# A routed feed-forward kernel: the activations of the first seven experts are computed in the routing block

## The reference, cut to what matters

```python
q = (xt @ w_q).reshape(n, PEER_HEADS, 2, PEER_DHALF)          # 8 heads
s = jnp.einsum('nhpd,hpkd->nhpk', q, keys)                    # 128 keys in each half
sv, si = lax.top_k(s, PEER_TOPK)                              # 16 best of each half
cand = sv[:, :, 0, :, None] + sv[:, :, 1, None, :]
cs, ci = lax.top_k(cand.reshape(n, PEER_HEADS, -1), PEER_TOPK)
gate = jax.nn.softmax(cs, axis=-1)
a = jnp.einsum('nd,nhkd->nhk', xt, u[eidx])
w = gate * jax.nn.gelu(a, approximate=False)
return jnp.einsum('nhk,nhkd->nd', w, v[eidx])
```

## Time and profile before

| what | us |
|---|---|
| median of three runs (lowest, highest) | 4531.56 (4529.86, 4535.65) |
| profiled execution, its own time | 4527.05 |
| its span, first to last instruction | 4525.2 |
| PE busy in the span | 4089.2 (90%) |
| DVE busy | 3006.6 (66%) |
| ACT busy | 2109.4 (47%) |
| POOL busy | 400.4 (9%) |

### The profile page before, as it was taken

The page is one execution under the profiler, slowest core; times in us unless marked ns, Lnnn a source line. Parts: engine busy times, 40 slices in busy tenths (PEclk is TensorE's granted clock), DMA queues, the critical chain, the costliest instruction groups (busy, mean ns, idle before and its releaser), DMA issues. The chain is left out here.

```text
span 4525.2 us, 71134 instructions
## 1 busy us (share of the span) xinstructions
PE 4089.2 (90%) x25056; PEld 3587.8 (79%) x25056; DVE 3006.6 (66%) x5888; ACT 2109.4 (47%) x3241; POOL 400.4 (9%) x470
## 2 busy tenths in 40 slices
PE   6997999959989677999999979999999769999998
PEld 5985889848977466888888868888888568888887
DVE  4555555555537649777777797777776688777776
ACT  4442444444434324555555545555554445555554
POOL 0000000000011015200000251000001044000000
PEclk9997999979989788999999989999999989999999
DMA  5554555554521031355555514555554121555554
GB/s 194 186 197 185 212 209 186 197 190 178 179 93 57 13 114 57 125 191 190 191 190 197 184 38 154 189 192 188 193 210 145 44 93 69 191 189 191 190 190 167
DMA packets 105284, 718.10 MB, mean 159 GB/s; under 512 B 13857, under 2 KB 14465, under 8 KB 21281
## 3 DMA queue, kind: packets, MB, share of 16 engines
q1 hardware_dynamic: 94688, 661.45, 40.8%
q0 software_dynamic: 8880, 52.12, 3.0%
q10 hardware_dynamic: 1552, 2.36, 0.2%
HBM read 709.48 MB, written 6.39 MB: 158 GB/s over the span
## 5 line engine op out<-in xcount | busy, mean ns | idle before, releaser
L228 DVE TENSOR_TENSOR units<-ring,units 128x1024 fp32r<-128x1024 f32 x1146 | 1390.5, 1224 | 535.9 <-ACT units L221 535.2
L221 ACT ACTIVATE units<-ring 128x1024 fp32r<-128x1024 f32 x1206 | 1272.8, 1056 | 959.3 <-PE ps L251 926.2
L3120 PE MATMUL ps<-wide,units 128*128 128x512 f32 x3072 | 759.0, 389 | 3.0 <-PEq L3018 3.0
L3120 PEld LDWEIGHTS ps<-wide,units 128*128 128x128 f32 x3072 | 576.3, 188 | 123.0 <-issue 3.5
L249 PE MATMUL ps<-units,weighted 128*128 128x512 f32 x1536 | 603.7, 393 | 8.7 <-DVE units L228 8.7
L250 PE MATMUL ps<-units,weighted 128*128 128x512 f32 x1536 | 603.0, 393 | 0.0
L251 PE MATMUL ps<-units,weighted 128*128 128x512 f32 x1536 | 598.2, 389 | 0.0
L3172 ACT ACTIVATE low_halves<-ps 128x256 f32<-128x256 f32 x384 | 147.7, 385 | 687.5 <-PE ps L3122 687.5
L3122 PEld LDWEIGHTS ps<-wide,units 128*128 128x128 f32 x3072 | 419.1, 190 | 29.9
L3122 PE MATMUL ps<-wide,units 128*128 128x256 f32 x3072 | 428.3, 282 | 0.0
L3190 DVE TENSOR_TENSOR gelued<-low_halves,ps 128x256 f32<-128x256 f32 x384 | 161.9, 421 | 377.6 <-ACT low_halves L3172 377.6
(11 more groups left out here) (497 smaller groups left out, 6504.3 us busy)
## 6 DMA issues: line engine op xcount, KB each, us to landing
ring<-in_stream SPq DMA_DIRECT2D x603, 1024.0 KB, 4.8
quad_ring<-in_mod_w POOLq DMA_DIRECT2D x12, 4096.0 KB, 14.1
front<-residuals_dram SPq DMA_DIRECT2D x5, 1024.0 KB, 7.0
gain_rows<-in_norm_gains SPq DMA_DIRECT2D x6, 512.0 KB, 4.5
peer_keys<-in_keys SPq DMA_DIRECT2D x3, 1024.0 KB, 5.1
ml_mask<-in_ml_mask SPq DMA_DIRECT2D x1, 2048.0 KB, 7.7
residuals_dram<-residual SPq DMA_DIRECT2D x2, 1024.0 KB, 6.7
front<-mod_rows_dram SPq DMA_DIRECT2D x4, 512.0 KB, 8.0
```

The source lines that it names most:

```text
L221: act.activation(K.parts(n)[0], K.raw(n), ACT.Copy).then_inc(K.sig("hi_made").sem, 1)
L228: dve.tensor_tensor(lo, K.raw(n), hi.bitcast(FP32), ALU.subtract).then_inc(K.sig("unit_split").sem, 1)
L3120: pe.matmul(both, hi[:, k, :], pair[:, :, k, :], start=(k == 0), stop=False)
```

## The change

The activations of experts 0 to 6 (`AHEAD` = 7) move from `experts` to `route`, behind PE's last scores. PE writes them to banks 2 and 3 in turn, now with 24 matmuls of 256 columns for each (`product3`) instead of 8 of 512 and 8 of 256. ACT copies each out of PSUM into the tile of the keys, which the scores no longer need (`take_early`), and applies Gelu to all seven at once into the ring slot that held u6 and u7 (`ahead_activations`). That slot stays taken through `spread_routes`. In `experts` DVE multiplies expert 0's activations as before and those of experts 1 to 6 with one instruction, in place in `G`; then SP may load the held slot again (`early_weighted`). The order of the stream becomes u0 to u7, v0 to v6, u8, v7, u9, v8, and so on. POOL splits six units more in `route`, ACT seven more; SP asks for three slots more there.

```diff
@@ route: @@
-                stream_weights(K, sp, PEER_HEADS)
+                stream_weights(K, sp, PEER_HEADS + AHEAD // 2)
...
-                for n in range(2, 2 * PEER_HEADS + 2):
+                for n in range(2, first_u + AHEAD + 1):
                     split_lo(K, pool, n0 + n)
+                pool.wait_ge(K.sig("unit_split").sem, n0 + first_u + AHEAD + 1)
...
                 score(PEER_HEADS - 1)
+                for e in range(AHEAD):
+                    n = n0 + first_u + e
+                    wait_unit(K, pe, n)
+                    if e >= 2:
+                        pe.wait_ge(*early_taken.at(e - 1))
+                    hi, lo = K.parts(n, kt=KD, cols=P)
+                    for k in range(KD):
+                        last = product3(pe, K.ps[:, 2 + e % 2, 0:SEQ], [hi[:, k, :], lo[:, k, :]],
+                                        [pair[:, h, k, :] for h in range(2)], k == 0, k == KD - 1)
+                    used(K, last)
...
+                def take_early(e):
+                    act.wait_ge(unit_used, n0 + first_u + e + 1)
+                    act.activation(early[:, e * SEQ:(e + 1) * SEQ], K.ps[:, 2 + e % 2, 0:SEQ], ACT.Copy)\
+                       .then_inc(early_taken.sem, 1)
...
+                split_hi(K, act, n0 + first_u + 2)
+                spread_numbers(5)
+                take_early(0)
+                split_hi(K, act, n0 + first_u + 3)
+                spread_numbers(6)
+                for e in (1, 2, 3):
+                    take_early(e)
+                    split_hi(K, act, n0 + first_u + 3 + e)
+                spread_numbers(7)
+                take_early(4)
+                split_hi(K, act, n0 + first_u + 7)
                 act.wait_ge(*diffs.at(1))
                 act.activation(wgt[:, :, :], wgt[:, :, :], ACT.Exp).then_inc(exped.sem, 1)
+                take_early(5)
+                split_hi(K, act, n0 + first_u + 8)
+                take_early(6)
+                act.wait_ge(*early_taken.at(AHEAD))
+                act.wait_ge(K.sig("unit_split").sem, n0 + first_u + AHEAD + 1)
+                act.activation(ahead_activations(K, K.taken + PEER_HEADS), early[:, 0:AHEAD * SEQ].rearrange(
+                    "p (e n) -> p e n", e=AHEAD), ACT.Gelu).then_inc(K.sig("early_gelued").sem, 1)
@@ experts: @@
 def u_unit(e):
-    return max(2 * e - 1, 0)
+    return e if e <= AHEAD else 2 * e - 1
...
 def v_unit(e):
-    return min(2 * e + 2, 2 * KEYS - 1)
+    return AHEAD + 1 + e if e < AHEAD else min(2 * e + 2, 2 * KEYS - 1)
...
+def ahead_activations(K, slot):
+
+    return K.slot(slot + AHEAD // 2)[:, 0:AHEAD * SEQ].rearrange("p (e n) -> p e n", e=AHEAD)
...
+                sp.wait_ge(*early_weighted.at(1))
                 stream_weights(K, sp, KEYS - 12)
...
+                activations(pe, AHEAD)
+                for e in range(AHEAD):
+                    outputs(pe, e)
                 steps(pe, step)
...
+                def split_early(e):
+                    if e >= 2:
+                        dve.wait_ge(unit_used, n0 + v_unit(e - 2) + 1)
+                    dve.tensor_copy(weighted[:, e % 2, 0, :], G[:, e, :]).then_inc(weights_made.sem, 2)
+                    dve.wait_ge(weights_made.sem, weights_made.base + STEPS * e + 2)
+                    dve.tensor_tensor(weighted[:, e % 2, 1, :], G[:, e, :], weighted[:, e % 2, 0, :].bitcast(FP32),
+                                      ALU.subtract).then_inc(weights_made.sem, 1)
...
+                split_lo(K, dve, n0 + v_unit(0))
+                split_product(dve, whole[:, 0, :], weighted[:, 0, :, :], early[:, 0, :], G[:, 0, :], weights_made, 0, 0)
+                dve.tensor_tensor(G[:, 1:AHEAD, :], early[:, 1:AHEAD, :], G[:, 1:AHEAD, :], ALU.mult)\
+                   .then_inc(early_weighted.sem, 1)
+                dve.wait_ge(*early_weighted.at(1))
+                split_early(1)
+                split_lo(K, dve, n0 + v_unit(1))
+                add_halves(AHEAD)
+                split_early(2)
+                split_lo(K, dve, n0 + v_unit(2))
+                for e in range(3, AHEAD):
+                    split_lo(K, dve, n0 + v_unit(e))
+                    split_early(e)
+                dve.wait_ge(unit_used, n0 + v_unit(AHEAD - 2) + 1)
+                weigh(AHEAD)
+                split_lo(K, dve, n0 + u_unit(FIRST))
+                split_lo(K, dve, n0 + v_unit(AHEAD))
                 steps(dve, step)
```

More of the change, by code:

```diff
@@ L2875, in _, with spread_numbers @@
             def _(act):
+                early = keys[:, :, :].rearrange("p h k -> p (h k)")
+                def spread_numbers(c):
+                    act.wait_ge(*ranked.at(c + 1))
+                    for t in range(MT):
+                        last = act.activation(numbers[:, t, :, :, c * TOPK:(c + 1) * TOPK],
+                                              idx[:, t, 2 * c:2 * c + 2, :].unsqueeze(3)
+                                              .broadcast_to([P, 2, TOPK, TOPK]), ACT.Copy)
+                    last.then_inc(spread_ids.sem, 1)
+                def take_early(e):
+                    act.wait_ge(unit_used, n0 + first_u + e + 1)
+                    act.activation(early[:, e * SEQ:(e + 1) * SEQ], K.ps[:, 2 + e % 2, 0:SEQ], ACT.Copy)\
+                       .then_inc(early_taken.sem, 1)
                 head.scalar(act)
-                for step in range(PEER_HEADS + 4):
+                for step in range(PEER_HEADS + 1):
                     if step < PEER_HEADS:
@@ L2896, in _ @@
                            .then_inc(tables_made.sem, 1)
[L2897 to L2904, removed]
+                    if step >= 4:
+                        spread_numbers(step - 4)
+                split_hi(K, act, n0 + first_u + 2)
[9 more added lines that the diff above has]
+                split_hi(K, act, n0 + first_u + 7)
                 act.wait_ge(*diffs.at(1))
                 act.activation(wgt[:, :, :], wgt[:, :, :], ACT.Exp).then_inc(exped.sem, 1)
+                take_early(5)
[5 more added lines that the diff above has]
+                    "p (e n) -> p e n", e=AHEAD), ACT.Gelu).then_inc(K.sig("early_gelued").sem, 1)
                 for t in range(MT):
@@ L2992, in route @@
     diffs.past(1), exped.past(1), weighed.past(1), found.past(2 * MT), turned.past(MT), copied.past(1)
+    early_taken.past(AHEAD), K.sig("early_gelued").past(1)
 def spread_routes(K, routes, G):
@@ L3111, in experts, with count @@
         weighted = K.sbuf("weighted", [P, 2, 2, SEQ], FP32R, ctx=local)
+        def count(signal, e, i=0):
+            return signal.sem, signal.base + e - AHEAD + 1 + i * BODY
         def activations(pe, e, i=0):
@@ L3137, in steps @@
         def steps(eng, step):
-            for e in range(2):
-                step(e, 0)
             with eng.Fori(0, loops) as i:
-                for e in range(2, 2 + BODY):
+                for e in range(FIRST, FIRST + BODY):
                     step(e, i)
-            for e in range(2 + BODY * loops, KEYS):
+            for e in range(FIRST + BODY * loops, KEYS):
                 step(e, 0)
```

53 lines of the change are left out of this document (38 added, 15 removed).

## The result

| kernel | median us (lowest, highest), runs |
|---|---|
| before | 4533.60 (4529.86, 4540.05), 4 |
| changed | 4478.07 (4474.53, 4479.66), 4 |

The ratio is 0.988, with a 95% interval from 0.9866 to 0.9895: the changed kernel is faster by 1.2%, 55.5 us. Two more timings on the same chip as the kernel before gave 4478.25 against 4535.46 (57.2 us less) and 4479.13 against 4537.09 (58.0 less). The forecast was 4474.5, with a saving of 57.0; the mean of the three savings is 56.9.

What follows compares the result with a forecast made beforehand. PE was taken to bound the expert block and DVE's chain the routing. Saving 20.9 us in the block less 1.9 for the port wait gives 19.0 a call, 57.0 in three: 4531.56 to 4474.5 us, range 4463 to 4487.

Steps and rivals of the forecast that it cites:

- The expert block, 20.9 us a call: From S, the block's start on PE, to `outputs(126)`: 702.4 us falls to 681.5, saving 20.9 a call.
- The stall at `outputs(1)`: Start of the expert block: PE waits 0.65 us once, for DVE's low half of v1.
- The held slot: Ring slot holding the early activations: asked for at S+4.1, landed at S+8.9, v4 ready at S+11.3, wanted at S+14.4.
- The wait on POOL's sixth split, 1.9 us a call: End of the ranking: DVE's differences wait from 1752.15 to 1754.0 for POOL's split; bounds 0 to 2.4 us.
- What was held to cost nothing: In the routing, PE's early activations, ACT's added work and the ranking beside POOL's splits were expected not to lengthen it.
- a slow clock in the early activations: PE at 1.2 GHz in the routing's early activations: routing 13.5 us longer, net 7.4 a call, 4509 us; chance 0.05.
- a slowed ranking: POOL's splits hold up DVE's ranking: 14.5 us a call at most, net 6.4, 4512 us; chance 0.02.
- a longer step: Expert block: ring never catches up, PE waits each step; a 5.8 us step would give 4579 us; chance 0.05.
- nothing left: The block's saving is lost in a routing 20 us longer: about 4531 us; chance 0.03.
- The sum: Whole kernel: 20.9 less 1.9 gives 19.0 us a call, 57.0 in three calls.

Runs made afterwards that it cites:

- e3: Changed kernel with expert 1 handled like expert 0 and its v split ahead of the large product: 4477.43 us, 0.9870 of the kernel before.
- e2: Changed kernel with five experts ahead instead of seven, so four more POOL splits than before instead of six: 4486.07 us, 0.9899 of the kernel before.
- b1_before_again: The kernel before, profiled once more with no edit: 4536.73 us in one run, span 4534.9.
- e1: Changed kernel with the operand of DVE's differences put into PSUM, so they read one SBUF operand: 4479.73 us, 0.9874 of the kernel before.
- the filler: Changed kernel with 32 matmuls whose results nobody reads, ahead of PE's wait for the gates: 4475.67 us, 0.9876 of the kernel before.

## Why the prediction was right, point by point

- **The expert block, 20.9 us a call.** 702.4 to 681.5 was expected and 702.39 to 681.41 was measured. `outputs(0)` starts at S+2.87 (2.76), DVE's split of v1 ends at S+6.02 (6.1), the large product takes 1.75 (1.76), and `activations(8)` starts at S+22.5 (22.7). The stall at `outputs(1)` is 0.44 by the starts of PE's rows, in place of 0.65. The held slot is asked for at S+4.4 (4.1) and nothing stalls behind it; e3 shows that a request 2 us later is too late.
- **The wait on POOL's sixth split, 1.9 us a call.** The mechanism is as forecast, with the split beginning 0.61 us ahead of the differences (0.55 expected). The size was 1.66, 1.31 and 1.67, mean 1.55, so the term of 1.9 was 0.35 too high. In the second call the split begins 0.97 us ahead, so less of it is left. e2, without such a split, has no wait and 1.7 us less.
- **What was held to cost nothing.** PE's early activations ran at 1.00, ended before the gates were ready, the exponentials waited for DVE, and the ranking took as long as before in two calls of three and 0.3 us longer in the second, by a wait whose cause is open. The rivals of a slow clock in the early activations, of a slowed ranking, of a longer step and of nothing left are out, each by the rows above. (The price that the forecast gave the slow clock, 13.5 us a call, doesn't follow from its own times, in which the gates alone come 18.3 us later.)
- **Terms the sum didn't have, of PE's clock.** The first costs: the last table row takes 3.60 instead of 2.20 us in some calls, 1.4 us each. The changed kernel has it in one call of three in each of three profiles. The kernel before has it too, in one call of six (b1_before_again, the last of the three timeline rows below). In the changed kernel it is the first call each time, while in both profiles of before the first call takes 2.20; whether the change has a part in it is open. The second gains: the kernel before waits 1.80 us for its first v, and behind that its products run slowly in some calls. In b1_before_again, PE's timeline in the first expert block and the last table row of the second call:

```profile
1860.28 0.66 PE L249 MATMUL ps<-units,weighted 128*128 128x512 f32 x1 [1.80 <-DVE units L228]
1860.75 0.63 PE L250 MATMUL ps<-units,weighted 128*128 128x512 f32 x1
...
2658.31 3.60 PE L2870 MATMUL ps<-peer_ident,gated 128*128 128x128 bf16 x32 [0.94 <-DVE gated L2986]
```

A window of that first expert block:

```profile
1862.00:1864.00 2.00, 2.00 (x6) 1.58 (x5) 1.76 (x4) 1.09 (x2) 0.00 (x0) 0.53 0.76 176
```

The granted clock is 0.53 there, near the 0.50 of 1.2 GHz. A product takes 0.63 us in place of 0.40, and the block is 708.0 us instead of 706.4. That is so in four of the six blocks of before that were profiled, and in none of the nine blocks of the changed kernel (685.4 to 685.5), whose stall is a quarter as long, here and in the other two profiles of it. The first trace of before had it only in the third call, on which the sum didn't look. It adds 1.6 us to the saving of such a call.

The third costs too: the stretch ahead of the third routing is 2.6 us longer, of which some 1.5 are the slow products in the windows above. The clock over these products is 0.50 to 0.52 in all three profiles of the changed kernel and 1.00 in both of before. Why the clock falls in products that the change doesn't touch is open. Between the copy of `routes` and the expert block another 1.2 us a launch are lost, 0.9 in the second call and 0.3 in the first, and the cause is open too: in the second call the clock is 0.50 at the start of `spread_routes` in the changed kernel, but 0.52 in b1_before_again as well, where the stretch isn't longer.
- **The sum.** From the first scores on, the profiles of the changed kernel are 56.8 us shorter than those of before on average (54.9 and 58.7 against the one and the other), as the medians say (55.5 to 58.0). Over the three calls, by the means of two profiles and of three: the expert blocks give 66.0, that is 62.8 as forecast and 3.2 from the slow products of before. The routings take 5.7: 4.6 for the port, 0.7 for the last table row, 0.3 in the second ranking. 1.2 are lost ahead of the expert blocks and 2.3 ahead of the second and third routing. That is 56.8. The forecast had 62.7 and 5.7, the two terms that it worked out, and both mechanisms are shown. That its total of 57.0 is met to within 1 us is luck: the 3.2 us that it lacked on the one side, and the port's 1.1 that it had too much, make up for the 4.5 that it lacked on the other.

## What to carry to other kernels

Work moved into an engine's idle time costs what it does to the engine on the critical path there. Here that was one 2.4 us split on POOL lying across DVE's first instructions after the ranking, 1.55 us a call out of a gain of 21. Look at what the bounding engine issues just when the moved work ends, and count the operands in SBUF of each of those instructions, and of the next ones too, since a wait that is taken off one may pass to the next, as in e1. And look at all executions of a stretch, not only the first: its price may be different in each. Where the median scatters by as much as an edit is worth, compare the profiles from a mark behind the scattering stretch on, the untouched stretches too: here they lost 3.5 us.

## What the runs showed of the hardware

- DVE's differences (128x256, two SBUF inputs) took 1.73 to 2.10 us beside a POOL split and 0.43 alone. A DVE shift with one SBUF input (128x256, uint32) took 1245 ns beside a POOL split and 280 alone. With the input in PSUM four of them took 1.41 us beside a split, without a wait. DVE's ranking instructions (maximum, index, replace) showed no lengthening: a MAX8 over 128 columns took 285 ns in the median before, 284 and 293 in two profiles after with six more splits, and the ranking takes as long as before in two calls of three.
- Reading from PSUM isn't free: those four shifts take 0.89 us from SBUF, which ate 0.5 of the 1.55 us that was saved, and the fifth, with no split beside it, 0.42 in place of 0.30.
- The granted clock fell to half behind idle time of only 1.80 us in four of six cases, and held in two, in the same kernel at the same place. With PE idle 3.84 us before the gates, the first table rows took 3.00 to 3.60 us in place of 2.20, and the second rows 2.20 or 3.60. With the filler, behind 2.34 us of idle time, the second rows took 2.88 to 3.36 in five of nine cases and 2.20 in four. So a stall's price may be its length and up to 1.6 us more, differing from call to call.
